# High and low tokens side by side in one 512-column product, the halves added by VectorE

## The reference, cut to what matters

```python
def swiglu(h, w_gate, w_up, w_down):
    return (jax.nn.silu(h @ w_gate) * (h @ w_up)) @ w_down

# layer 0
h = rms_norm(x, ffn_norm[0])
x = x + swiglu(h, ffn_w_gate[0], ffn_w_up[0], ffn_w_down[0])
...
# second block
h = rms_norm_2(x, pre_mlp_norm)
m = square(relu(h @ w_up)) @ w_down      # 1024 -> 4096 -> 1024
x = x + rms_norm_2(m, post_mlp_norm)
```

## Time and profile before

| | us |
|---|---|
| median of 3 | 1800.59 |
| profiled execution | 1803.72 |
| its span | 1801.9 |
| TensorE matmul busy | 1703.9 |
| VectorE busy | 1272.4 |
| ScalarE busy | 985.6 |
| first feed-forward, up products from | 156.5 |
| its last down product ends | 345.0 |
| second feed-forward | 1609 to 1790 |

### The profile page before, as it was taken

One profiled execution on the slowest core, in us unless ns is written; L12 is line 12 of the kernel. 1 busy time (PEld: TensorE's weight loads), 2 busy tenths in 40 slices (PEclk: granted clock), 3 DMA queues, 4 the chain that ended last, 5 costly groups with the idle time before them and its releaser, 6 DMA issues.

```text
span 1801.9 us, 24579 instructions
## 1 busy us (share of the span) xinstructions
PE 1703.9 (95%) x9718; PEld 1493.2 (83%) x9718; DVE 1272.4 (71%) x1306; ACT 985.6 (55%) x1071; POOL 16.2 (1%) x22
## 2 busy tenths in 40 slices
PE   6988999898989999999999999999969999979998
PEld 5867999797878888888888888888859989969997
DVE  4964444545369898888888898988878477555554
ACT  3333444445357777777777776777755441344443
POOL 1000000000000000000000000000000000000000
PEclk9999999899969999999999999999989899989999
DMA  6404554533119898988989898989964300035550
GB/s 267 152 0 187 187 187 164 187 140 141 40 60 373 333 351 323 368 338 347 371 316 369 328 352 331 362 317 372 354 259 164 140 2 1 1 140 187 187 187 24
DMA packets 31189, 401.48 MB, mean 223 GB/s; under 512 B 3688, under 2 KB 3952, under 8 KB 5520
## 3 DMA queue, kind: packets, MB, share of 16 engines
q1 hardware_dynamic: 30704, 399.44, 58.6%
q0 software_dynamic: 416, 1.06, 0.2%
HBM read 399.43 MB, written 1.06 MB: 222 GB/s over the span
## 4 chain that ended last, share of the span: by engine, by line
PE 80%; DVE 8%; DMA 5%; ACT 4%; issue 3%; SPq 0%; DVEq 0%; ACTq 0%
PE ps L1845 21%; PE ps L1847 21%; PE ps L1846 21%; DMA raw<-in_ws 4%; PE ps L1903 3%; DVE wl L876 2%; PE ps L2351 2%; ACT wh L871 2%; PE ps L1919 2%; PE ps L2004 2%; PE ps L2339 1%; PE ps L2161 1%; DMA ring<-in_ws 1%; PE ps L2151 1%; DVE wl L762 1%
## 5 line engine op out<-in xcount | busy, mean ns | idle before, releaser
L876 DVE TENSOR_TENSOR wl<-raw,wh 128x2048 fp32r<-128x2048 f32 x266 | 607.8, 2290 | 90.7 <-ACT wh L871 87.7
L871 ACT ACTIVATE wh<-raw 128x2048 fp32r<-128x2048 f32 x264 | 506.4, 1919 | 200.7 <-PE ps L1847 82.3
L1845 PE MATMUL ps<-wh,f_r 128*128 128x512 f32 (+1 forms) x1200 | 461.3, 384 | 8.9 <-DVE wl L876 6.3
L1846 PE MATMUL ps<-wl,f_r 128*128 128x512 f32 (+1 forms) x1200 | 455.2, 379 | 0.0
L1847 PE MATMUL ps<-wh,f_r 128*128 128x512 f32 (+1 forms) x1136 | 430.3, 379 | 0.0
L1845 PEld LDWEIGHTS ps<-wh,f_r 128*128 128x128 f32 x1200 | 227.0, 189 | 53.7 <-DVE wl L876 9.2
L1846 PEld LDWEIGHTS ps<-wl,f_r 128*128 128x128 f32 x1200 | 227.2, 189 | 40.8
L1845 PE MATMUL ps<-ht_t_r,wh 128*128 128x256 f32 x832 | 241.0, 290 | 8.8 <-DVEq L655 6.6
L1847 PEld LDWEIGHTS ps<-wh,f_r 128*128 128x128 f32 x1136 | 214.3, 189 | 40.4
L1847 PE MATMUL ps<-ht_t_r,wl 128*128 128x256 f32 x832 | 239.8, 288 | 0.0
L1846 PE MATMUL ps<-h_t_r,wh 128*128 128x256 f32 x832 | 238.6, 287 | 0.0
(11 more groups left out here) (406 smaller groups left out, 2017.5 us busy)
## 6 DMA issues: line engine op xcount, KB each, us to landing
raw<-in_ws SPq DMA_DIRECT2D x169, 2048.0 KB, 9.0
raw<-in_ws SPq DMA_DIRECT2D x25, 1024.0 KB, 5.2
ring<-in_ws SPq DMA_DIRECT2D x6, 2048.0 KB, 11.2
gb<-in_gains SPq DMA_DIRECT2D x5, 512.0 KB, 8.5
x_t<-in_x SPq DMA_DIRECT2D x1, 1024.0 KB, 5.0
f<-scratch POOLq DMA_DIRECT2D x8, 128.0 KB, 3.0
out<-x_t SPq DMA_DIRECT2D x2, 512.0 KB, 2.6
cst<-in_const SPq DMA_DIRECT2D x1, 964.5 KB, 6.9
```

Source lines behind the costliest of these rows:

```text
L871: nc.scalar.activation(half_of(wh, h % SPLIT), raw_half(h % HALVES), ACT.Copy).then_inc(S("high"), 1)
L876: nc.vector.tensor_tensor(half_of(wl, h % SPLIT), raw_half(h % HALVES), half_of(wh, h % SPLIT).bitcast(F32), ALU.subtract).then_inc(S("spl ...
L1845: first = nc.tensor.matmul(bank, xh, h, start=start, stop=False)
L1846: nc.tensor.matmul(bank, xh, l, start=False, stop=False)
```

## The change

The high and low tokens now lie in one tensor `hh` (low first, then high), so that chunk c of both is a moving operand of 2 x 256 columns, `LOHI[:, c]`. `features_wide` takes the high weights once, against low and high tokens side by side, 512 columns wide (L1889), and the low weights against the high tokens in 256 columns (L1888, L1893), which go into the upper half of the bank. So each group of 128 features needs a bank of its own, whose lower half holds high by low and whose upper half holds high by high plus low by high. VectorE adds the two halves of a bank with a reduction over two elements (`both_parts`, L771) and writes the sum to `SGF` in SBUF. Silu then reads SBUF, the product in the first feed-forward has both inputs in SBUF, and in the second Relu and square become one VectorE instruction. A unit now uses two of the four banks instead of one.

```diff
--- before.py
+++ after.py
@@ -183,8 +183,8 @@
         wh = sb("wh", SPLIT * HALF, F32R)
         wl = sb("wl", SPLIT * HALF, F32R)
         x_t = sb("x_t", TT * D)
-        h_t, h_r = sb2("h_t", TT * D)
-        ht_t, ht_r = sb2("ht_t", DC * SEQ)
+        hh, hh_r = sb2("hh", TT * D + DC * SEQ)
+        (h_t, ht_t), (h_r, ht_r) = ([a[:, k * TT * D:(k + 1) * TT * D] for k in range(2)] for a in (hh, hh_r))
         big, big_r = sb2("big", 8192)
         f1, f1_r = sb2("f1", 2048)
         f2, f2_r = sb2("f2", 2048)
@@ -253,7 +253,8 @@
         plan_four(pre, "wout")
         plan_norm(pre, 1)
         for i in range(FT):
-            pre.add_at(("ff", i), i % 4)
+            for k in range(2):
+                pre.add_at(("ff", i, k), 2 * (i % 2) + k)
         for tt in range(TT):
             for c in range(2):
                 pre.add_at(("ffd", tt, c), 4 + 2 * tt + c)
@@ -331,7 +332,8 @@
             post.add(("og", tt))
         plan_norm(post, 7)
         for i in range(FT2 // 2):
-            post.add_at(("up", i), i % 4)
+            for k in range(2):
+                post.add_at(("up", i, k), 2 * (i % 2) + k)
         for tt in range(TT):
             for c in range(2):
                 post.add_at(("mlp", tt, c), 4 + 2 * tt + c)
@@ -383,7 +385,8 @@
         PRF = big[:, 2048:3072].rearrange("p (b n) -> p b n", b=2)
         SGF = big[:, 3072:4096].rearrange("p (b n) -> p b n", b=2)
         NH = mid_r[:, 0:DC * (HEADS + 2 * GH)]
-        HT1 = Pair(ht_r[:, :], h_r[:, :], "tcs")
+        HT1 = Pair(ht_r[:, :], h_r[:, :])
+        LOHI = hh_r[:, :].rearrange("p (k c s) -> p c k s", k=2, s=SEQ)
         HTQ = Pair(ht_r[:, :], f1_r[:, :])
         HTK = Pair(f3_r[:, :], h_r[:, :], "tcs")
         MA = Pair(ht_r[:, 0:1024], ht_r[:, 1024:2048])
@@ -762,15 +765,21 @@
             nc.vector.tensor_tensor(half_of(wl, h % SPLIT), half_of(raw, 2 * (n % RAW) + part),
                                     half_of(wh, h % SPLIT).bitcast(F32), ALU.subtract).then_inc(S("b_split"), 1)
 
+        def both_parts(dve, B, name, dst):
+
+            bank = filled(dve, B, name)
+            ins = nc.vector.tensor_reduce(dst, bank[:, :].rearrange("p (k s) -> p s k", k=2), AX, ALU.add)
+            return let_go(B, name, ins)
+
         def ffn_act(act):
 
             for s in range(FT // 2):
                 for i in (2 * s, 2 * s + 1):
-                    bank = filled(act, pre, ("ff", i))
-                    nc.scalar.activation(SGF[:, i % 2, 0:SEQ], bank[:, 0:SEQ], ACT.Silu).then_inc(S("f_silu"), 1)
+                    b, k = pre.at[("ff", i, 0)]
+                    act.wait_ge(pre.free[b], k + 1)
+                    nc.scalar.activation(SGF[:, i % 2, 0:SEQ], SGF[:, i % 2, 0:SEQ], ACT.Silu).then_inc(S("f_silu"), 1)
                     high_pre(act)
-                    b, k = pre.at[("ff", i)]
-                    act.wait_ge(pre.free[b], k + 1)
+                    act.wait_ge(S("f_prod"), i + 1)
                     nc.scalar.activation(ATH[:, s % 2, i % 2, :], PRF[:, i % 2, 0:SEQ], ACT.Copy).then_inc(S("f_ath"), 1)
                 if s:
                     high_pre(act)
@@ -779,11 +788,13 @@
 
             for s in range(FT // 2):
                 for i in (2 * s, 2 * s + 1):
-                    bank = filled(dve, pre, ("ff", i))
+                    both_parts(dve, pre, ("ff", i, 0), SGF[:, i % 2, 0:SEQ])
+                    low_pre(dve)
+                    free, n = both_parts(dve, pre, ("ff", i, 1), SGF[:, i % 2, SEQ:2 * SEQ])
+                    dve.wait_ge(free, n)
                     dve.wait_ge(S("f_silu"), i + 1)
-                    ins = nc.vector.tensor_tensor(PRF[:, i % 2, 0:SEQ], bank[:, SEQ:2 * SEQ], SGF[:, i % 2, 0:SEQ], ALU.mult)
-                    let_go(pre, ("ff", i), ins)
-                    low_pre(dve)
+                    nc.vector.tensor_tensor(PRF[:, i % 2, 0:SEQ], SGF[:, i % 2, SEQ:2 * SEQ], SGF[:, i % 2, 0:SEQ],
+                                            ALU.mult).then_inc(S("f_prod"), 1)
                     dve.wait_ge(S("f_ath"), i + 1)
                     nc.vector.tensor_tensor(ATL[:, s % 2, i % 2, :], PRF[:, i % 2, 0:SEQ], ATH[:, s % 2, i % 2, :].bitcast(F32),
                                             ALU.subtract).then_inc(S("f_at"), 1)
@@ -796,9 +807,6 @@
         def mlp_act(act):
 
             for s in range(FT2 // 2):
-                bank = filled(act, post, ("up", s))
-                ins = nc.scalar.activation(SGF[:, s % 2, :], bank[:, :], ACT.Relu)
-                let_go(post, ("up", s), ins)
                 if todo["high_post"] < 2 * N_POST:
                     high_post(act)
                 act.wait_ge(S("m_square"), s + 1)
@@ -809,9 +817,11 @@
         def mlp_dve(dve):
 
             for s in range(FT2 // 2):
-                b, k = post.at[("up", s)]
-                dve.wait_ge(post.free[b], k + 1)
-                nc.vector.tensor_tensor(PRF[:, s % 2, :], SGF[:, s % 2, :], SGF[:, s % 2, :], ALU.mult).then_inc(S("m_square"), 1)
+                for k in range(2):
+                    free, n = both_parts(dve, post, ("up", s, k), SGF[:, s % 2, k * SEQ:(k + 1) * SEQ])
+                    dve.wait_ge(free, n)
+                nc.vector.scalar_tensor_tensor(PRF[:, s % 2, :], SGF[:, s % 2, :], 0.0, SGF[:, s % 2, :],
+                                               ALU.max, ALU.mult).then_inc(S("m_square"), 1)
                 if todo["low_post"] < 2 * N_POST:
                     low_post(dve)
                 dve.wait_ge(S("m_ath"), s + 1)
@@ -1865,6 +1875,25 @@
                 closed(B, name, ins)
                 half_used(B)
 
+            def features_wide(B, names, ready=None):
+
+                h, l = (t.rearrange("p (c n) -> p c n", c=DC) for t in half_unit_of(B))
+                for i in range(2):
+                    bank = opened(pe, B, names[i])
+                    for c in range(DC):
+                        if ready and i == 0:
+                            ready(c)
+                        hc, lc = h[:, c, i * P:(i + 1) * P], l[:, c, i * P:(i + 1) * P]
+                        if c:
+                            nc.tensor.matmul(bank[:, SEQ:2 * SEQ], lc, LOHI[:, c, 1], start=False, stop=False)
+                        ins = nc.tensor.matmul(bank[:, :].rearrange("p (k s) -> p k s", k=2), hc, LOHI[:, c], start=c == 0, stop=c == DC - 1)
+                        if c == 0:
+                            if i == 0:
+                                pay(ins)
+                            nc.tensor.matmul(bank[:, SEQ:2 * SEQ], lc, LOHI[:, c, 1], start=False, stop=False)
+                    closed(B, names[i], ins)
+                half_used(B)
+
             def tokens(B, names, pair, c0, begin, end):
 
                 h, l = (t.rearrange("p (c n) -> p c n", c=4) for t in half_unit_of(B))
@@ -2023,7 +2052,7 @@
             norm_pe(pe, pre, 1, 2)
             for s in range(FT // 2):
                 for i in (2 * s, 2 * s + 1):
-                    features(pre, ("ff", i), HT1, (lambda c: lows_ready(1, c)) if i == 0 else None)
+                    features_wide(pre, [("ff", i, k) for k in range(2)], (lambda c: lows_ready(1, c)) if i == 0 else None)
                 if s:
                     pe.wait_ge(S("f_at"), 2 * s)
                     down(pre, "ffd", s - 1, FT // 2)
@@ -2440,7 +2469,7 @@
 
             norm_pe(pe, post, 7, 6)
             for s in range(FT2 // 2):
-                features(post, ("up", s), HT1, (lambda c: lows_ready(7, c)) if s == 0 else None)
+                features_wide(post, [("up", s, k) for k in range(2)], (lambda c: lows_ready(7, c)) if s == 0 else None)
                 if s:
                     pe.wait_ge(S("m_at"), s)
                     down(post, "mlp", s - 1, FT2 // 2)
```

## The result

The changed kernel takes 1811.83 us, median of 5 runs (1809.72 to 1815.75), against 1800.59 us for the kernel before (5 runs, 1795.73 to 1803.39): ratio 1.0069, 95% interval 1.0048 to 1.0090. It is slower, by 11.2 us; 1812 was forecast.

The account below looks back on a forecast made before the run. TensorE bounds both stages before; after the change the ScalarE-VectorE dance bounds the first feed-forward. 13.8 + 0.7 - 3.4 = +11.1 us, forecast 1812 us against the median, range 1803 to 1820.

Parts of the forecast that it names:

- TensorE's saving: Up halves of both feed-forwards: 16 fewer matmuls at 13 ns save 0.21 us each, 8.1 us if TensorE stays the bound.
- The reduction: VectorE's new sum of 512 PSUM elements to 256 (L771) takes 0.69 us, bounds 0.28 and 1.22.
- B: Rival, chance 0.06: VectorE's reduction costs by its 256 outputs, 0.42 us; loop 16.9 us a step, total 1800.4 us.
- C: Rival, chance 0.07: reducing pairs 256 elements apart costs double, 1.22 us; total 1835 us.
- The loop: First feed-forward: ScalarE and VectorE work in turn, 17.97 us a step against TensorE's 16.53, so they become the bound.
- Rival A: Chance 0.05: in the first feed-forward TensorE stays the bound, loop under 16.53 us; -8.1 us, total 1792.5 us.
- Rival E: Chance 0.02: the wide product gains nothing because its moving operand comes from two places; total 1815 us.
- The end of the stage: First feed-forward: TensorE idles about 9 us ahead of the last down product, part of +13.8 us for all waits.
- the cold clock: Last down product of the first feed-forward starts at 1.2 GHz, loses 1.6 us; about half shows, +0.7 us.
- Rival D: Chance 0.04: TensorE's waits of about 1.4 us a step lower its clock within first feed-forward steps; total 1817 us.
- one to two times a step: Profile sign, first feed-forward: how often TensorE would wait for low weights (L746), 1.4 us together.
- the second stage's saving: Second feed-forward: TensorE stays the bound, 16 up halves save 0.21 us each, -3.4 us.

Follow-up runs that it names:

- e10: e3 with all 8 wide products of a group first, then its 8 narrow ones, instead of one by one: 1788.35 us, ratio 0.9935 to the kernel before.
- e2: Only the second feed-forward changed, the first put back as in the kernel before: 1798.23 us, ratio 0.9986 to the kernel before.
- e4: Changed kernel; in the first feed-forward a VectorE copy of 256 elements replaces each reduction, lower bank half left out: 1801.58 us, ratio 1.0002 to the kernel before.
- e5: Changed kernel; in the first feed-forward VectorE does the gate bank's reduction twice, once into a spare tile: 1824.35 us, ratio 1.0144 to the kernel before.
- e3: Changed kernel; in the first feed-forward VectorE makes the low weights behind the second reduction and product: 1792.00 us, ratio 0.9948 to the kernel before.
- e9: Changed kernel; in the first feed-forward ScalarE makes the high weights ahead of Silu, VectorE's order kept: 1795.20 us, ratio 0.9969 to the kernel before.
- e8: e3 with the wide product reading 512 adjacent elements instead of twice 256 in two places: 1790.98 us, one execution.

## Why the prediction was right

*TensorE's saving.* Forecast 0.21 us per up half from 13 ns per matmul; measured 0.16 to 0.17 (5.755 to 5.59). The forecast took 0.2265 us from 17 products in the middle of a down half and used it for every wide product, but the earlier trace rows begin where the slower ones behind narrow products are over, and in the new up half each wide product stands behind a narrow one (e10). In the second stage that is -2.8 instead of -3.4 us (e2). The price of 2.5 ns per matmul, which the Trainium skill gives (TensorE: Matmul & The Clock Gate, section "Wait — 56ns, not 53.3ns?"), would be 0.04 us per half and 0.6 us in the second stage, by an estimate. The runs are nearer to the rows, with 10 ns.

*The reduction.* 0.69 taken from the rows for 512 inputs, 685 ns measured over 76:

```profile
L771 DVE TENSOR_REDUCE big<-ps 128x256 f32<-128x512 f32 x76 | 52.0, 685 | 14.2 <-PE ps L1889 14.2
```

It goes by inputs; pairs 256 elements apart cost nothing more. Rivals B and C fall. The loop of e4 is what B's number would have given, and it gave it: 1800.4 was worked out for B, 1801.6 measured.

*The loop.* 17.97 us a step forecast, 17.97 measured. E4 and e5 move the step by just what is put in or taken out, e3 and e9 cut a link each and bring back TensorE's own 16.63. Rival A, TensorE as the bound, came true with e3 and e9, and in the kernel as changed it did not. Rival E fell too: the wide product gains (e2), and its two places cost nothing (e8).

*The end of the stage.* "About 9 us" of idling ahead of the last down product, 8.5 measured; +13.8 us for waits and end together and +0.7 for the cold clock, +14.6 measured for all. The last down product's first matmul before is this one:

```profile
339.37 0.39 PE L1845 MATMUL ps<-wh,big_r 128*128 128x512 f32 x1
```

(The prediction put it at 339.5.) From the first up product to it are 182.87 us before and 197.05 after, +14.2; from it to the square 6.14 before (339.37 to 345.51) and 6.54 after, +0.4. Of the 2 us that the nine products at 1.2 GHz lose, only the first one's longer record shows (0.79 for 0.39 us), because the high weights, behind them the low ones and behind these the additions wait for that product; the prediction had said about half of the loss. Rival D did not occur: the clock was at 1.00 from 160 to 345 us, and TensorE's waits of 0.9 to 1.0 us between matmuls did not lower it. But its mechanism is real, as e5 with waits of 1.9 us shows.

*Where it was off.* TensorE waits for low weights seven times, not "one to two times a step": once in each step from the fifth on, the first at 224.65, with weight loads up to 1.3 us late, 8.8 us in all. Up to then, I take it, the weights that were made ahead last; no run shows that apart. The prediction had that begin after two or three steps. The two stages come to +11.8 us where the sum said +11.1, as the second stage's saving was forecast 0.6 us too large. That the median fell on the forecast within 0.2 us is luck beyond the 1 us to which the stages agree: the untouched part alone moves by 6.7 us from profile to profile.

## What to carry to other kernels

Two engines that take turns through queues in fixed order can be half idle and yet be the bound: write down the loop (who waits for whom within a unit, and for the next unit) and add it up against the engine that bounds the stage. When work moves from one engine to another, it is less its length that counts than whether it stands ahead of or behind the long instruction in that queue; here two places further down, behind the second reduction and the product, were worth 18 us in the stage (e3). An instruction on which another engine waits goes ahead of the one that nobody needs soon.

## What the runs showed of the hardware

- A product of 256 fp32r columns takes 0.119 to 0.120 us, one of 512 takes 0.2265, and 0.230 behind products of 256 (e10). Joining two of 256 saved about 10 ns of a pair; reading from two places costs nothing (e8).
- After 8.5 us of idling TensorE ran nine products of 512 columns at 1.2 GHz, in 4.0 us. In the changed kernel waits of 0.9 to 1.0 us between matmuls, every 18 us, left the clock at 1.00; in e5 three of five waits of 1.9 us were followed by a stretch at 1.2 GHz.
- The untouched part between the stages took 1255.2 to 1261.9 us in twelve profiles, shortest where TensorE spent the least time at 1.2 GHz in it (78 to 79 us of up to 97). What decides that was not tried. A gain of 0.2% in a stage is seen in the stage's own events in one profile, but hardly in the total.
